# Two VectorE operations that add the bias and keep the row maximum, in the attentions of layer 1

## The reference, cut to what matters

```python
def windowed_attend(q, k, v, k_ctx, v_ctx, sink):          # C
    s_loc = jnp.where(valid, einsum(q, kb), NEG)
    s_ctx = einsum(q, k_ctx)
    p = jax.nn.softmax(jnp.concatenate([sk, s_ctx, s_loc], axis=-1), axis=-1)
    ...
def neighborhood_attend(q, k, v, k_ctx, v_ctx, rpb):       # D
    s_loc = einsum(qg, kg) + bias
    s_loc = jnp.where(col_valid, s_loc, NEG)
    s_ctx = einsum(qg, k_ctx)
    p = jax.nn.softmax(jnp.concatenate([s_ctx, s_loc], axis=-1), axis=-1)
```

## Time and profile before

| | us |
|---|---|
| median of 3 runs (lowest, highest) | 1677.62 (1676.86, 1682.78) |
| the profiled execution, its own time | 1677.31 |
| its span in the trace | 1675.5 |
| PE busy / DVE busy / ACT busy / POOL busy | 1536.0 / 904.1 / 677.0 / 157.7 |
| layer 1, attention C | 1304 to 1397 |
| layer 1, attention D | 1397 to 1441 |

### The profile page before, as it was taken

One profiled execution on the slowest core, in us unless ns is written; L12 is line 12 of the kernel. 1 busy time (PEld: TensorE's weight loads), 2 busy tenths in 40 slices (PEclk: granted clock), 3 DMA queues, 4 the chain that ended last, 5 costly groups with the idle time before them and its releaser, 6 DMA issues.

```text
span 1675.5 us, 24174 instructions
## 1 busy us (share of the span) xinstructions
PE 1536.0 (92%) x9546; PEld 1307.6 (78%) x9546; DVE 904.1 (54%) x1513; ACT 677.0 (40%) x1095; POOL 157.7 (9%) x121
## 2 busy tenths in 40 slices
PE   7999899999999568998898999999998988869997
PEld 7998698998987455785688777777787776768886
DVE  6776744544546684436764433333457645555444
ACT  4553444444444324425554222222234534444442
POOL 3100400000000300000014001111002020021110
PEclk9999999999999788999999999999999999979999
DMA  6456555344436123411111543543413510224451
GB/s 247 160 201 227 207 204 201 132 171 140 163 128 229 56 76 151 152 51 51 75 65 62 201 155 147 201 175 140 188 51 110 167 64 1 109 112 176 182 200 52
DMA packets 43338, 233.75 MB, mean 140 GB/s; under 512 B 13088, under 2 KB 14048, under 8 KB 16352
## 3 DMA queue, kind: packets, MB, share of 16 engines
q1 hardware_dynamic: 30944, 222.38, 35.4%
q10 hardware_dynamic: 12288, 9.88, 2.1%
HBM read 231.16 MB, written 1.08 MB: 139 GB/s over the span
## 4 chain that ended last, share of the span: by engine, by line
PE 79%; DVE 11%; ACT 5%; issue 3%; POOL 1%; DMA 1%; ACTq 0%; DVEq 0%; SPq 0%; POOLq 0%
PE ps L516 22%; PE ps L517 21%; PE ps L518 21%; PE ps L719 5%; DVE wlo L979 3%; PE ps L606 2%; PE ps L658 2%; ACT whi L969 2%; PE ps L692 2%; PE ps L650 1%; PE ps L568 1%; POOL flo L2106 1%; DVE nmax L1682 1%; PE ps L590 1%; DVE nmax L1710 1%
## 5 line engine op out<-in xcount | busy, mean ns | idle before, releaser
L979 DVE TENSOR_TENSOR wlo<-raw,whi 128x2048 fp32r<-128x2048 f32 x162 | 383.5, 2393 | 269.3 <-ACT whi L969 269.1
L516 PE MATMUL ps<-fhi,whi 128*128 128x256 f32 (+1 forms) x1280 | 391.3, 306 | 11.7 <-DVE wlo L979 7.2
L969 ACT ACTIVATE whi<-raw 128x2048 fp32r<-128x2048 f32 x162 | 303.8, 1905 | 231.9 <-PE ps L518 177.6
L518 PE MATMUL ps<-fhi,wlo 128*128 128x256 f32 (+1 forms) x1280 | 387.7, 303 | 0.0
L517 PE MATMUL ps<-flo,whi 128*128 128x256 f32 (+1 forms) x1280 | 387.6, 303 | 0.0
L516 PEld LDWEIGHTS ps<-fhi,whi 128*128 128x128 f32 x1280 | 246.4, 192 | 34.5 <-issue 10.3
L518 PEld LDWEIGHTS ps<-fhi,wlo 128*128 128x128 f32 x1280 | 246.3, 192 | 8.9
L517 PEld LDWEIGHTS ps<-flo,whi 128*128 128x128 f32 x1280 | 246.4, 193 | 8.7
L516 PE MATMUL ps<-whi,fhi 128*128 128x512 f32 (+1 forms) x592 | 208.3, 352 | 7.4 <-DVE e_b L1937 3.8
L517 PE MATMUL ps<-wlo,fhi 128*128 128x512 f32 (+1 forms) x592 | 205.2, 347 | 0.0
L518 PE MATMUL ps<-whi,flo 128*128 128x512 f32 (+1 forms) x592 | 205.1, 346 | 0.0
(11 more groups left out here) (220 smaller groups left out, 1823.8 us busy)
## 6 DMA issues: line engine op xcount, KB each, us to landing
raw<-in_wstream SPq DMA_DIRECT2D x210, 1024.0 KB, 4.9
gates<-gated ACTq DMA_DIRECT2D x6, 512.0 KB, 4.5
hx<-in_x SPq DMA_DIRECT2D x1, 1024.0 KB, 5.7
lnrow<-in_ln_g ACTq DMA_DIRECT2D x2, 512.0 KB, 4.2
lnrow<-in_ln_b ACTq DMA_DIRECT2D x2, 512.0 KB, 5.6
hc<-in_ctx ACTq DMA_DIRECT2D x1, 1024.0 KB, 4.8
mix<-in_rpb_rows ACTq DMA_DIRECT2D x4, 256.0 KB, 4.9
hc<-in_rpb_rows ACTq DMA_DIRECT2D x4, 256.0 KB, 3.7
```

The costliest lines, as they stand in the source:

```text
L516: mm(o, lh, rh, start=start, stop=False)
L518: return mm(o, ll, rh, start=False, stop=stop)
L969: nc.scalar.activation(whi[:, w % SPLIT_SLOTS, :], raw[:, c % RAW_SLOTS, :], ACT.Copy).then_inc(*did("scalar", ("hi", w)))
L979: nc.vector.tensor_tensor(wlo[:, w % SPLIT_SLOTS, :], raw[:, c % RAW_SLOTS, :], whi[:, w % SPLIT_SLOTS, :].bitcast(F32), ALU.subtract).the ...
```

## The change

In `maxima` for the kinds C and D, the addition, the copy and the maximum over 512 columns become two `tensor_tensor_reduce` operations over 256 columns each, which write the biased scores to `e_b` and leave the maximum of what they wrote in `half_max`, and one `reduce_max` over these two values. The second one adds a new tile `zero`, 128 x 1, read with step 0 along the columns. The wait between the two big operations and the `reduce_max` stays. The first model's attention (kind `first`) keeps its own `reduce_max`.

```diff
+        zero = tile(ctx, "zero", [P, 1])
+        half_max = tile(ctx, "half_max", [P, ITEMS_KEPT, 2])
...
+            v.memset(zero[:, :], 0.0).then_inc(*did("vector"))
...
                     a = src("s", it, 0)
-                    v.tensor_tensor(e[:, 0:S], a[:, 0:S], band[:, t, :] if kind == "C" else bias_d(h, t), ALU.add).then_inc(
-                        *did("vector", ("biased", it)))
-                    link(v.tensor_copy(e[:, S:2 * S], a[:, S:2 * S]), ("read", "s", it, 0))
-                ins = v.reduce_max(nmax[:, i % ITEMS_KEPT, 0:1], e[:, 0:kt * P], AX_X, negate=True)
+                    m = half_max[:, i % ITEMS_KEPT, :]
+                    v.tensor_tensor_reduce(e[:, 0:S], a[:, 0:S], band[:, t, :] if kind == "C" else bias_d(h, t), 1.0, MASKED,
+                                           ALU.add, ALU.max, m[:, 0:1]).then_inc(*did("vector"))
+                    link(v.tensor_tensor_reduce(e[:, S:2 * S], a[:, S:2 * S], heads_view(zero[:, 0:1], (0, S)), 1.0, MASKED,
+                                                ALU.add, ALU.max, m[:, 1:2]), ("read", "s", it, 0))
+                    ins = v.reduce_max(nmax[:, i % ITEMS_KEPT, 0:1], m, AX_X, negate=True)
+                if kind == "first":
+                    ins = v.reduce_max(nmax[:, i % ITEMS_KEPT, 0:1], e[:, 0:kt * P], AX_X, negate=True)
```

## The result

The change makes the kernel faster: 1664.53 us, the median of 4 runs (1663.67 to 1666.31), against 1677.53 (1676.86 to 1682.78) before. The ratio is 0.9911, with a 95% interval of 0.9891 to 0.9931. That is 13.0 us where 5.1 were forecast; the time lies under the predicted range. The profiled execution took 1666.31 us, with a span of 1664.5. In the later groups of runs the kernel before splits into executions at about 1677 to 1680 us and at 1682 to 1686, so that a ratio to them shows more gain than the traces do.

What follows compares the result with a forecast made beforehand. PE bounds the kernel (busy 1536 of 1675.5 us), so DVE savings pay only where PE waits for them: 4.1 + 0.25 + 0.75 = 5.1 us off 1677.31 gives 1672.2; range 1668.5 to 1678.

Steps and rivals of the forecast that it cites:

- The operation: In maxima: new operations 0.34 us from start to start, small reduction 0.16; one item gains 0.51 us.
- the loop: In D: PE, DVE and ACT wait in a 5.11 us cycle per pair, containing only the first item's maxima.
- D: Attention stretch with nothing else beside it: eight pairs by 0.51 give 4.1 us, the last gap 0.25.
- Rival 1: In maxima: keeping operation at half rate for 256 columns, kernel about 2.2 us slower, 1679.5; chance 0.08.
- rival 2: In D: something else holds PE's gap, only the start of C gains, 1676.5 us; chance 0.05.
- rival 4: In maxima: dearer writes and reduction, about 3.6 us gained, 1673.7; chance 0.16 together with small clock shifts.
- C's start: Where C begins: PE's 0.98 us wait for p_b shrinks, as that copy starts earlier; 0.75 us gained.
- The middle of C: PE's 4.45 us stall at 1367 keeps its place, as DVE's small minimum ends with POOL; nothing gained.
- the prediction's own list: Signs against it: streaming operation over 0.5 us, D's gap staying at 1.1, or a changed stall in mid C.
- the list of what the change does: Whole kernel: shorter maxima, a memset left at nothing (0.1 us if not), later work shifting forward; 5.1 us in all.
- all shifts forward: Behind the attention, from 1440 us on: weights follow PE, so the gain lasts to the end.
- Rival 3: Middle of C: stall under POOL and the low clock after it go away, 6.1 us more, 1666; chance 0.06.

Runs made afterwards that it cites:

- e1_edit_only: The change as it is, but its two new tiles lie where nothing stands behind them, against the kernel before: 1673.37 us, ratio 0.9955.
- e2_place96: The kernel before with only an unused tile of 96 bytes per partition where the change puts its two tiles: 1674.04 us, ratio 0.9957.
- e8_sink_scalar: The changed kernel with the small minimum with the sink as a tensor_scalar, the sink a per-partition scalar: 1663.58 us, ratio 0.9885 to the kernel before.
- e6_d_first: The kernel before with the new operations only in the first item of each D pair, no other tile moved: 1675.01 us, ratio 0.9949.
- e7_d_second: The kernel before with the new operations only in the second item of each D pair, no other tile moved: 1677.97 us, ratio 0.9982.
- e10_weights32: The kernel before with whi and wlo moved by 32 bytes, fhi and all behind it by 128: 1680.38 us, ratio 1.0.
- e4_place64: The kernel before with an unused tile of 64 bytes per partition where the change puts its two tiles: 1678.61 us, ratio 1.0.

## Why the prediction was wrong

**The operation, the loop and D: right.** New operations of 0.42 us at a distance of 0.35, a small reduction of 0.16, 1.00 us in place of 1.51, a gap of 0.60, a pair every 4.61: each as forecast. D was to give 4.1 + 0.25 and gave 4.1 + 0.41. Rival 1 (the keeping operation dear), rival 2 (the gap held by something else) and rival 4 (partial gain) did not come: the price taken from two operations at 64 columns held at 256 and with a PSUM source.

**C's start: right in kind, the term too large.** 0.75 forecast, 0.42 found, in the kernel after and in `e1_edit_only`. The prediction let `prob_copy` start 0.53 us after the transposes began. ACT's timeline of the kernel after:

```profile
1312.56 0.39 ACT L1148 ACTIVATE qT_b<-ps 128x256 f32<-128x256 f32 x1 [0.52 <-PE ps L520]
...
1313.22 0.60 ACT L1140 ACTIVATE p_b<-ps 128x512 f32<-128x512 f32 x1 [0.27 <-PE ps L694]
```

It started at 1313.22, 0.86 after the transposes' 1312.36, and ACT stood idle for 0.27 of that, waiting for them. The first four of eight transposes were put at 0.5 us, half of the group's 1.04; they are done, and seen by ACT, only after 0.86. That is the missing 0.33.

**The middle of C: the mechanism right, the zero not exact.** By the prediction's own list a change of this stall was to count against it. L1720 still ends with POOL (1353.54 + 2.33 = 1355.87; POOL 1355.86), as forecast, but after 2.33 us, not 2.8. In `e1_edit_only` it takes 2.63 and the stretch gains nothing. In the kernel after POOL started 0.5 us earlier against PE's work, since the last bias row landed that much sooner, and the gap shrank by 0.5 to 3.95. The gap shrank by 0.36 (to 4.09) in `e2_place96` too, which has none of the new operations, and by 0.18 (to 4.27) in `e1_edit_only`, which has all of them, so the 0.5 is how a load happened to land, not the edit.

**The step that failed: the list of what the change does.** It reads "the new memset ... is left at nothing" and "behind the attention ... all shifts forward", and has no term for the two new tiles as such. Their 96 bytes moved `hhi`, `hlo` and other tiles, and changed the distance between the starts of 1152 matmuls from a mean of 236 ns to 230 (waits included), far from the edit's place in the code. In the trace the two feed-forwards gave some 6 us by it, more than the 5.1 forecast for everything; alone, by ratio, it is 0.43% (0.28 to 0.57), where the whole forecast was 0.30%. In the terms of the forecast, the edit's own 5.1 us stands against 4.7 in the trace of `e1_edit_only`, whose 1673.37 us lies within the forecast's 1.5 us around 1672.2. "All shifts forward" held there within 0.6 us. The chance of 0.08 for "faster by over 0.5%" was low because no rival let a gain come from outside the attentions.

**Rival 3** gave a time near the one measured (1666), for a reason that did not happen: the stall stayed and the clock fell. Where `e8_sink_scalar` took the stall away, the clock fell all the same. That the measured time is nearer to rival 3 than to the forecast is chance.

**What stays open.** The runs show that the distance between the stationary and the moving tile sets the pace, not why, and not why 256 columns have another order. The 1.5 us by which the kernel after is behind at 890 us is put down to where short stretches of low clock fell, but no run isolates that; `e6_d_first` and `e7_d_second`, which move no tile, are 1.9 and 1.7 us behind there. The 3 us of the traces that neither half of the change has are open in the same way.

## What to carry to other kernels

Price an edit in the loop that PE waits in: an operation that keeps its maximum on the way costs no more than the plain one, and removing a reduction pays only for the item whose maximum is awaited. Count a new tile as part of the change: look up which tiles behind it move and by how much, and to learn what an edit is worth, allocate its tiles where nothing stands behind them. Where matmuls with 512 columns fill the engine, try an unused tile that puts the stationary and the moving operand on the same byte modulo 128; it costs one line. Measure it: with 256 columns the same byte was the slowest place here, and a tile that helps one group of matmuls can slow another, as in `e10_weights32`.

## What was not expected of the hardware

Matmuls of 512 float32 columns in reduced precision, one behind the other at full clock, start 227 ns apart when the moving and the stationary tile are on the same byte modulo 128, 231 to 237 (mean 233) when 32 apart, 226 to 232 (mean 229) at 64, and 234 (mean 233) at 96. Both tiles on multiples of 128, or both 32 past, have the same pace. The 96 of `hhi` in `e4_place64` and of `fhi` in `e10_weights32` are distances of 137696 and 65632 bytes, which agree modulo 128 and not modulo 256, and both have 234 ns. In this kernel it is worth about 6 us of 1677.

An instruction on 128 x 1 elements with two SBUF inputs stood for the rest of POOL's operation (2.33 us); the same minimum with a per-partition scalar took 0.21.
